# Reordering the mixing stage of a hybrid encoder layer: gate units, state-space steps and GLU units

## The chip, the cores and the metric

The kernel runs on one core of a Trainium2 chip. The metric is the device time of one execution in microseconds. One core has a matrix engine (PE, TensorE), a vector engine (DVE, VectorE), an activation engine (ACT, ScalarE), a general engine (POOL, GpSimd) and a sync engine (SP) that only starts transfers. Each engine runs its own list of instructions in order, and they wait for each other through semaphores, which are counters.

## The reference

One layer works on x of 1024 tokens by 1024 features: a SwiGLU block, a mixing block, a cross-attention and a second SwiGLU block. Only the order inside the mixing block is changed. Cut to what matters:

```python
u = rms_norm(h); p, s, g_pool, g_ssm = split(u @ w_in)      # 512 | 256 | 1024 | 1024
z_pool = (stack_g(pool_minus_self(p[g], window[g]) @ pool_w[g]) * pool_scale) @ w_pool_proj   # 4 groups of 128
y_ssm  = gelu(bidirectional_S5(s))                           # 16 groups of 16 channels, 64 complex states
z_ssm  = (y_ssm @ w_glu_val) * sigmoid(y_ssm @ w_glu_gate)
merged = sigmoid(g_pool) * z_pool + sigmoid(g_ssm) * z_ssm
h = h + merged @ w_mix_out
```

Here pool_minus_self is a centred mean over 2, 4, 8 or 16 tokens less the token itself, and S5 is a linear recurrence forwards and backwards in time.

## The kernel before, in words

Everything is kept transposed, features on the 128 partitions and 1024 tokens along each row. A float32 product is made of three products of shortened parts: weight high by data high, weight high by data low, weight low by data high (`three`, L523 is the matmul in the helper `mm`). A **unit** is one 128x1024 block of weights: SP loads it, POOL splits it into `w_hi` (L1114) and `w_lo` (L1116), and PE runs 48 matmuls of 512 columns with it. There are three slots for split units, so POOL splits a unit as soon as PE has finished the one three before it.

The result of a product goes to one of four PSUM pairs (`take_pair`). PE counts its products, and product k waits until the pair of product k-4 has been read. The readers free the pairs in the order of the products, so DVE must take the products in the order in which PE makes them (`wait_product`).

The mixing block runs in this order on PE:

- four units that make s and the first two groups of p (`opening` and one more);
- the pooled products `pool_mix(g)`, six matmuls each with the data that DVE's `pool(g)` has built by shifted sums, with three units between them: the last two groups of p and the first gate unit (a gate unit is one of eight that make g_pool). DVE scales and splits each result in `pool_mixed(g)`;
- eight steps over pairs of SSM groups. In step q PE runs `ssm_states(q)` (small matmuls on `u_t` and `e_m`), a gate unit, and `ssm_out(q)` (small matmuls on `sx` and `f_m`). Beside the gate unit DVE turns the states and scans them into `sx`. After `ssm_out(q)` DVE copies the result to `y_t`, ACT stores it and starts the six loads of step q+2 (`load_step`) into one of two sets of tables. The last step has a `pool_proj` in place of a gate unit, and three more follow. These loads and the store are issued on ACT's own queue;
- the GLU part, four times: one GLU unit (gate and value products for two of the eight output tiles, four products of 12 matmuls) and two units of g_ssm. DVE and ACT bring them together in `merged`;
- the eight units of w_mix_out, which read `merged` split into `ua_hi` (ACT) and `ua_lo` (DVE), tile by tile. The first of them waits for each tile.

`wait_dve()` on PE or ACT waits for the next count that DVE passes on; `first(tally)` is a tiny memset by which DVE passes one on once its earlier work is done. `link` makes each DVE instruction wait for the one before it.

Of the kernel before, what the change touches and what calls it, by code (L numbers as in the profile page):

```python
# [5 lines left out]
F32 = mybir.dt.float32  # L6
# [5 lines left out]
P = 128  # L12
# [22 lines left out]
KV_BUFFER = (0, 1, 2, 3, 0, 1, 2, 3, 0, 1, 2, 4, 0, 1, 2, 4)  # L35
KP, FP, MP = KT // 2, FT // 2, KT // 2

INV_2PI = float(np.float32(1 / (2 * np.pi)))
# [186 lines left out]
def build(nc, a):  # L225
    ctx = ExitStack()
    with ctx:
# [44 lines left out]
        with ExitStack() as v:  # L272
            merged_again, z_a, z_b, z_c, z_d = tensors(v, [
                ("merged_again", [P, KT, L], F32), ("z_a", [P, 2, L], F32), ("z_b", [P, 2, L], F32),
                ("z_c", [P, L], F32), ("z_d", [P, L], F32)])
        ub_hi, ub_lo = tensors(ctx, [("ub_hi", [P, KT, L], F32R), ("ub_lo", [P, KT, L], F32R)])
# [239 lines left out]
        def _(pe):  # L516
# [326 lines left out]
            def pool_mix(g):  # L843
                pair = take_pair()
                wait_dve()
                three(pair, pw_hi[:, g], pw_lo[:, g], pooled[:, g % 2, 0], pooled[:, g % 2, 1], True, True,
                      HALVES, done=True)

            def ssm_states(q):
# [11 lines left out]
            def ssm_out(q):  # L861
# [4 lines left out]
                for gg in range(2):  # L866
# [15 lines left out]
            pool_mix(3)  # L882

# [6 lines left out]
            for q in range(PAIRS):  # L890
                ssm_states(q)
                if q + 1 < PAIRS:
                    unit_product(ua_hi, ua_lo)
                else:
                    pool_proj()
                ssm_out(q)
            for j in range(1, KT // 2):
                pool_proj()
            wait_dve()
            for j in range(KT // 2):  # L900
                whi, wlo = take_unit()
# [6 lines left out]
                unit_product(ua_hi, ua_lo)  # L908
                unit_product(ua_hi, ua_lo)
            for m in range(KT):  # L910
# [361 lines left out]
        def _(act):  # L1272
# [378 lines left out]
            gate(0)  # L1651
            wait_dve()
            load_step(1)
            for q in range(PAIRS):
                if q + 1 < PAIRS:
                    gate(q + 1)
                wait_dve()
# [13 lines left out]

            for m in range(KT):
                if m % 2 == 0:
                    for m2 in range(2):
                        run(z_b[:, m2], finished_product("glu gate", m + m2)[:].rearrange("p c n -> p (c n)"), ACT.Sigmoid)
                if m == KT - 1:
                    wait_dve()
                    for k in range(5):
                        high(k)
                one(z_d[:], z_c[:], ACT.Sigmoid)  # L1680
            for m in range(5, KT - 1):
                high(m)
            wait_dve()
            high(KT - 1)
            for m in range(KT):
# [62 lines left out]
        def _(dve):  # L1748
# [647 lines left out]
            def pool(g):  # L2396
# [16 lines left out]
                stt(nxt[:, PAD:PAD + L], cur[:, PAD:PAD + L], 1.0 / w, mx_v[:, PAD:PAD + L], ALU.mult, ALU.subtract)  # L2413
                hi, lo = pooled[:, g % 2, 0], pooled[:, g % 2, 1]
                cp(hi, nxt[:, PAD:PAD + L])
# [22 lines left out]

            gate(0)
            link(v.memset(sx[:], 0.0))  # L2440
            dve.wait_ge(s_uld, 16 * T)
            for q in range(PAIRS):
                dve.wait_ge(s_step[q % 2], 96 * (q // 2 + 1))
                tab = step_sets[q % 2][3]
                first(to_pe)
                if q == 0:
                    pool_mixed(2)
                    pool_mixed(3)
                    first()
                    wait_act()  # L2450
                pair = wait_product()
# [20 lines left out]

                if q + 1 < PAIRS:
                    gate(q + 1)
                else:
                    project(0)
                    project(1)
                pair = wait_product()
# [3 lines left out]
                first()  # L2482
                if q + 1 < PAIRS:
                    wait_act()
            for m in range(2, KT):
                if m == KT - 2:
                    wait_act()
                    cp(y_hi[:], y_g[:])
                    tt(y_lo[:], y_g[:], y_hi[:].bitcast(F32), ALU.subtract, tally=to_pe)
                project(m)  # L2490

            def merged_low(m):
# [3 lines left out]

            for m in range(KT):
                if m % 2 == 0:
                    for m2 in range(2):
                        wait_product()  # L2500
                        wait_act()
                        first(free)
                        tt(z_a[:, m2], wait_product(), z_b[:, m2], tally=free)
                pair = wait_product()
                if m == KT - 1:
                    first()
                tt(z_c[:], pair, rn[:], tally=free)
                first()
                if m == KT - 1:
                    for k in range(5):  # L2510
                        merged_low(k)
                wait_act()
                tt(z_d[:], z_d[:], z_a[:, m % 2])
                tt(merged[:, KT - 1 - m], merged[:, KT - 1 - m], z_d[:], ALU.add)
            first()
            for m in range(5, KT):
                merged_low(m)
            dve.wait_ge(s_hload, 16 * KT)
# [145 lines left out]
```

## Time and profile before

| | us |
|---|---|
| median of 3 runs | 2156.42 |
| lowest and highest run | 2152.35, 2160.49 |
| the profiled execution, its own time | 2166.18 |
| its span in the profile | 2164.4 |
| PE busy in the span | 2064.8 (95%) |
| DVE, ACT, POOL busy | 1422.5 (66%), 637.9 (29%), 1218.7 (56%) |

The profiled execution is 9.8 us longer than the median of the runs, and 1.8 us of its time lie outside the span. Times of single instructions come from this execution, counted from the start of the span. The mixing block lies between about 750 and 1246 us.

### The profile page before, as it was taken

To read this page: it belongs to the slowest core of one execution; us is meant where nothing else is said; L and a number is where in the kernel's file an instruction comes from. 1 tells how busy PE (TensorE), PEld (TensorE's weight loads), DVE (VectorE), ACT (ScalarE), POOL (GpSimd) and SP (SyncE) were. 2 spreads that over 40 slices of the span, in tenths; PEclk is the share of its full clock that TensorE was granted. 3 is DMA by queue.
4 is the path that set the end of the run, shared out by engine and by line. 5 is a ranking of instruction groups with operands and counts; after the bars stand their busy time and mean duration, and the time that the engine had idled before them with its cause. 6 is when DMAs were issued, how large, how long until landed. Compare 5 with 4: busy or idle time off the path is not lost.

```text
span 2164.4 us, 24480 instructions
## 1 busy us (share of the span) xinstructions
PE 2064.8 (95%) x9194; PEld 1685.0 (78%) x9194; DVE 1422.5 (66%) x1611; ACT 637.9 (29%) x979; POOL 1218.7 (56%) x802
## 2 busy tenths in 40 slices
PE   8899999999989989999998999899899999999996
PEld 4787778788878877778886888787788888887785
DVE  6677667566776979453334265546677776787778
ACT  5422322233344410001112123324232322234442
POOL 6388687778555532212332431035699998985551
PEclk9999999999999999999999999999999999999998
DMA  6423332347767462332113141111223223267763
GB/s 262 141 95 109 130 133 74 103 140 286 268 223 250 146 172 62 90 98 61 49 49 117 49 160 65 69 58 59 73 93 105 95 93 127 93 223 263 259 213 136
DMA packets 140628, 286.37 MB, mean 132 GB/s; under 512 B 12384, under 2 KB 37600, under 8 KB 140128
## 3 DMA queue, kind: packets, MB, share of 16 engines
q1 hardware_dynamic: 100496, 233.21, 31.7%
q10 hardware_dynamic: 40016, 51.61, 7.4%
q8 instruction: 74, 1.21, 0.2%
q14 instruction: 42, 0.34, 0.0%
HBM read 222.39 MB, written 63.42 MB: 132 GB/s over the span
## 4 chain that ended last, share of the span: by engine, by line
PE 61%; DVE 23%; DMA 6%; issue 4%; POOL 3%; ACT 1%; SPq 1%; DVEq 0%; ACTq 0%; POOLq 0%
PE ps L523 60%; DMA raw<-in_dn 4%; DVE w_lo L2341 3%; DVE xt_lo L2331 3%; DVE f_g L1778 2%; DVE h L2350 2%; DMA d_act<-f_g 1%; DVE acc L1778 1%; DVE sq L2144 1%; POOL w_lo L1106 1%; POOL start_room L1202 1%; DVE ua_lo L1778 1%; DVE sq L2327 1%; DVE sq L2182 1%; POOL raw L1185 1%
## 5 line engine op out<-in xcount | busy, mean ns | idle before, releaser
L1106 POOL TENSOR_TENSOR w_lo<-raw,w_hi 128x512 fp32r<-128x512 f32 x352 | 550.7, 1580 | 221.0 <-ACT w_hi L1341 220.7
L523 PE MATMUL ps<-xt_hi,w_hi 128*128 128x512 f32 x1320 | 517.9, 392 | 12.8 <-DVE xt_lo L2331 11.3
L523 PE MATMUL ps<-xt_lo,w_hi 128*128 128x512 f32 x1320 | 514.1, 389 | 0.0
L523 PE MATMUL ps<-xt_hi,w_lo 128*128 128x512 f32 x1320 | 514.0, 389 | 0.0
L1341 ACT ACTIVATE w_hi<-raw 128x512 fp32r<-128x512 f32 x462 | 278.6, 626 | 534.0 <-POOL raw L1134 269.9
L1114 POOL TENSOR_SCALAR w_hi<-raw 128x1024 fp32r<-128x1024 f32 x54 | 61.4, 1136 | 511.1 <-PE ps L523 504.0
L523 PEld LDWEIGHTS ps<-xt_hi,w_hi 128*128 128x128 f32 x1320 | 248.2, 188 | 75.0 <-issue 20.1
L523 PEld LDWEIGHTS ps<-xt_hi,w_lo 128*128 128x128 f32 x1320 | 248.1, 188 | 52.0
L523 PEld LDWEIGHTS ps<-xt_lo,w_hi 128*128 128x128 f32 x1320 | 248.3, 188 | 50.4
L1134 POOL TENSOR_TENSOR raw<-raw 128x512 f32<-128x512 f32 x178 | 274.6, 1552 | 12.9 <-DMA raw<-in_gu 5.6
L523 PE MATMUL ps<-ua_hi,w_hi 128*128 128x512 f32 x608 | 242.2, 398 | 10.9 <-DVE ua_lo L1778 7.0
L1185 POOL TENSOR_TENSOR raw<-raw 128x512 f32<-128x512 f32 x110 | 164.9, 1509 | 145.1 <-DMA raw<-in_dn 145.0
L523 PE MATMUL ps<-ua_lo,w_hi 128*128 128x512 f32 x608 | 239.9, 394 | 0.0
L523 PE MATMUL ps<-xb_hi,w_hi 128*128 128x512 f32 x528 | 209.1, 396 | 9.7 <-ACT f_g L1434 4.0
L523 PE MATMUL ps<-xb_lo,w_hi 128*128 128x512 f32 x528 | 208.1, 394 | 0.0
L523 PE MATMUL ps<-xb_hi,w_lo 128*128 128x512 f32 x528 | 208.0, 394 | 0.0
L2144 DVE TENSOR_TENSOR f_g<-ps,f_g 128x512 f32<-128x512 f32 x158 | 109.2, 691 | 144.2 <-ACT f_g L1434 119.8
L523 PE MATMUL ps<-ua_hi,w_lo 128*128 128x512 f32 x608 | 189.0, 392 | 0.0
L1116 POOL TENSOR_TENSOR w_lo<-raw,w_hi 128x1024 fp32r<-128x1024 f32 x54 | 145.9, 2702 | 4.5
L523 PEld LDWEIGHTS ps<-ua_hi,w_hi 128*128 128x128 f32 x608 | 116.6, 192 | 39.4 <-DVE ua_lo L1778 5.3
L2341 DVE TENSOR_TENSOR w_lo<-raw,w_hi 128x512 fp32r<-128x512 f32 x110 | 108.8, 989 | 56.2 <-ACT w_hi L1341 55.7
L523 PEld LDWEIGHTS ps<-ua_lo,w_hi 128*128 128x128 f32 x608 | 116.5, 192 | 23.9
(310 smaller groups left out, 2907.6 us busy)
## 6 DMA issues: line engine op xcount, KB each, us to landing
raw<-in_dn SPq DMA_DIRECT2D x264, 256.0 KB, 3.6
raw<-in_gu SPq DMA_DIRECT2D x88, 512.0 KB, 5.6
raw<-in_weights SPq DMA_DIRECT2D x54, 512.0 KB, 3.5
d_act<-acc SPq DMA_DIRECT2D x20, 512.0 KB, 2.8
d_act<-sq SPq DMA_DIRECT2D x20, 512.0 KB, 3.8
d_act<-f_g SPq DMA_DIRECT2D x20, 512.0 KB, 4.6
h<-in_x SPq DMA_DIRECT2D x16, 512.0 KB, 9.1
xt_hi<-d_act SPq DMA_DIRECT2D x8, 1024.0 KB, 7.0
```

The lines of the kernel that those rows point to most:

```text
L523: ins = nc.tensor.matmul(out, lhsT, rhs, start=start, stop=stop)
L1106: add(lo, src, hi.bitcast(F32), op=ALU.subtract).then_inc(s_w_low["pool"], 1)
L1114: nc.gpsimd.tensor_scalar(hi, src, 1.0, 0.0, ALU.mult, ALU.add).then_inc(s_w_hi, 1)
L1116: add(lo, src, hi.bitcast(F32), op=ALU.subtract).then_inc(s_w_low["pool"], 1)
L1134: add(out, x, y, op=op).then_inc(s_w_sum, 1)
L1185: add(raw_part(op, 0), raw_part(op, 0), raw_part(op, 1), op=ALU.add if w[2] > 0 else ALU.subtract).then_inc(s_w_sum, 1)
L1341: nc.scalar.activation(w_hi[:, op.halves[0]].rearrange("p k c -> p (k c)"), src, ACT.Copy).then_inc(s_w_high, 1)
L1778: link(v.tensor_tensor(out, x, y, op), tally)
L2144: link(v.tensor_tensor(out, x, y, ALU.add), adds)
L2331: v.tensor_tensor(xt_lo[:, 3, d % 4], acts_at(d // FP, d % FP), xt_hi[:, 3, d % 4].bitcast(F32), ALU.subtract).then_inc(s_a_lo, 1)
L2341: v.tensor_tensor(lo, raw_part(op, 0), hi.bitcast(F32), ALU.subtract).then_inc(s_w_low["dve"], 1)
L2350: v.scalar_tensor_tensor(out=x, in0=bank, scalar=0.5 * sign, in1=x, op0=ALU.mult, op1=ALU.add).then_inc(s_dev, 1)
```

## The change

It moves instructions and waits; the arithmetic is the same but for the order in which three factors of z_ssm are multiplied. Part by part:

- A unit is put ahead of `pool_mix(0)`, and the second gate unit and `ssm_states(0)` ahead of `pool_mix(3)`. Between the four pooled products PE now has one unit, one unit, and one unit with the small states product. DVE's order follows: `pool(2)` comes before `pool_mixed(0)`, and `pool_mixed(3)` beside step 0.
- `ssm_states(q)` waits for the loads of its step (and `u_t` for q = 0) and for its PSUM pair. The wait for DVE is gone, and with it the count that DVE passed on at the start of each step.
- Gate units run two ahead, so steps 6 and 7 both have a `pool_proj`, and two more follow instead of three. ACT issues the loads of step 1 when `pool_mix(3)` has ended.
- In the GLU part the two units of g_ssm come before the GLU unit, and the packed weights follow. The sigmoid of g_ssm is kept in place (`z_c`), then multiplied by the sigmoid of the GLU gate, then by the value product.
- The high and low splits of `merged` tiles 0 to 3 are put among the work of the last GLU unit.

The diff, cut to its core:

```diff
-        mix += [("glu", j), ("w_in", 14 + 2 * j), ("w_in", 15 + 2 * j)]
+        mix += [("w_in", 14 + 2 * j), ("w_in", 15 + 2 * j), ("glu", j)]
...
             def ssm_states(q):
...
-                wait_dve()
+                if q == 0:
+                    pe.wait_ge(s_uld, 16 * T)
+                pe.wait_ge(s_step[q % 2], 96 * (q // 2 + 1))
...
+            unit_product(ua_hi, ua_lo)
             pool_mix(0)
             unit_product(ua_hi, ua_lo)
             pool_mix(1)
             unit_product(ua_hi, ua_lo)
+            pool_mix(2)
             unit_product(ua_hi, ua_lo)
-            pool_mix(2)
+            ssm_states(0)
             pool_mix(3)
...
             for q in range(PAIRS):
-                ssm_states(q)
-                if q + 1 < PAIRS:
+                if q:
+                    ssm_states(q)
+                if q + EARLY_GATES < KT:
                     unit_product(ua_hi, ua_lo)
                 else:
                     pool_proj()
                 ssm_out(q)
-            for j in range(1, KT // 2):
+            for j in range(EARLY_GATES, KT // 2):
                 pool_proj()
-            wait_dve()
             for j in range(KT // 2):
+                unit_product(ua_hi, ua_lo)
+                unit_product(ua_hi, ua_lo)
+                if j == 0:
+                    wait_dve()
...
             gate(0)
-            wait_dve()
+            act.wait_ge(s_prod, finished["pool mix", 3])
             load_step(1)
...
-            pool(0)
-            pool(1)
+            for g in range(3):
+                pool(g)
             pool_mixed(0)
-            pool(2)
+            pool(3)
             pool_mixed(1)
-            pool(3)
...
-                first(to_pe)
-                if q == 0:
-                    pool_mixed(2)
-                    pool_mixed(3)
...
+            for j in range(KT // 2):
+                last = j == KT // 2 - 1
+                for m2 in range(2):
+                    tt(z_c[:, m2], wait_product(), rn[:], tally=free)
+                    first()
+                for _ in range(2):
+                    wait_act()
+                for m2 in range(2):
+                    m = KT - 1 - (2 * j + m2)
+                    if last:
+                        for k in range(2 * m2, 2 * m2 + 2):
+                            merged_low(k)
+                    wait_product()
+                    wait_act()
+                    first(free)
+                    tt(z_b[:, m2], z_b[:, m2], z_c[:, m2])
+                    tt(z_a[:, m2], wait_product(), z_b[:, m2], tally=free)
+                    tt(merged[:, m], merged[:, m], z_a[:, m2], ALU.add)
...
+            for k in range(4, KT):
+                merged_low(k)
```

On PE at the end of the pooled products, before. The rows are the end of a gate unit (`ua_hi`, `ua_lo`), `pool_mix(2)` and `pool_mix(3)` (`mx_pooled`), `ssm_states(0)` (`u_t`, `e_m`) and the start of the next gate unit:

```order
L523 MATMUL ps<-ua_hi,w_lo 128x512 x2
L523 MATMUL ps<-mx_pooled,pw_hi 128x512 [waits dve_for_pe,psum_pair_free]
L523 MATMUL ps<-mx_pooled,pw_hi 128x512 x3
L523 MATMUL ps<-mx_pooled,pw_lo 128x512 x2
L523 MATMUL ps<-mx_pooled,pw_hi 128x512 [waits dve_for_pe,psum_pair_free]
L523 MATMUL ps<-mx_pooled,pw_hi 128x512 x3
L523 MATMUL ps<-mx_pooled,pw_lo 128x512 x2
L523 MATMUL ps<-u_t,e_m 64x128 [waits dve_for_pe,psum_pair_free]
L523 MATMUL ps<-u_t,e_m 64x128 x7
L523 MATMUL ps<-ua_hi,w_hi 128x512 [waits psum_pair_free,w_lo_written_by_pool]
```

The same place of the change, from the end of the second gate unit:

```order
L524 MATMUL ps<-ua_hi,w_lo 128x512 x2
L524 MATMUL ps<-u_t,e_m 64x128 [waits ssm_step_loaded0,u_loaded,psum_pair_free]
L524 MATMUL ps<-u_t,e_m 64x128 x7
L524 MATMUL ps<-mx_pooled,pw_hi 128x512 [waits dve_for_pe,psum_pair_free]
L524 MATMUL ps<-mx_pooled,pw_hi 128x512 x3
L524 MATMUL ps<-mx_pooled,pw_lo 128x512 x2
L524 MATMUL ps<-ua_hi,w_hi 128x512 [waits psum_pair_free,w_lo_written_by_pool]
```

`pool_mix(2)` and `pool_mix(3)` stood together; now a gate unit and the states product stand between them.

On PE between two steps, before: the end of `ssm_out(0)` (`sx`, `f_m`), then `ssm_states(1)`:

```order
L523 MATMUL ps<-u_t,m_m 128x128
L523 MATMUL ps<-sx,f_m 128x128 x4
L523 MATMUL ps<-u_t,e_m 64x128 [waits dve_for_pe,psum_pair_free]
L523 MATMUL ps<-u_t,e_m 64x128 x7
L523 MATMUL ps<-ua_hi,w_hi 128x512 [waits psum_pair_free,w_lo_written_by_pool]
```

The same place of the change:

```order
L524 MATMUL ps<-u_t,m_m 128x128
L524 MATMUL ps<-sx,f_m 128x128 x4
L524 MATMUL ps<-u_t,e_m 64x128 [waits ssm_step_loaded1,psum_pair_free]
L524 MATMUL ps<-u_t,e_m 64x128 x7
L524 MATMUL ps<-ua_hi,w_hi 128x512 [waits psum_pair_free,w_lo_written_by_pool]
```

The order is the same and the wait for DVE has become a wait for the step's loads.

On DVE at the end of the GLU part, before. `z_c` is the last unit of g_ssm, `ua_lo` the low split of a `merged` tile, and the first row of `h` belongs to the products of w_mix_out:

```order
L1838 MEMSET stat 128x1 [waits product_done,dve_step]
L1778 TENSOR_TENSOR z_c<-ps,rn 128x1024 [waits dve_for_act]
L1838 MEMSET stat 128x1 [waits psum_pair_free]
L1778 TENSOR_TENSOR ua_lo<-merged,ua_hi 128x1024 [waits act_for_dve,dve_for_act]
L1778 TENSOR_TENSOR ua_lo<-merged,ua_hi 128x1024 [waits act_for_dve,dve_for_pe] x4
L1778 TENSOR_TENSOR z_d<-z_d,z_a 128x1024 [waits act_for_dve,dve_for_pe]
L1778 TENSOR_TENSOR merged<-merged,z_d 128x1024 [waits dve_step]
L1838 MEMSET stat 128x1 [waits dve_step]
L1778 TENSOR_TENSOR ua_lo<-merged,ua_hi 128x1024 [waits act_for_dve,dve_for_act]
L1778 TENSOR_TENSOR ua_lo<-merged,ua_hi 128x1024 [waits act_for_dve,dve_for_pe] x2
L2018 SCALAR_TENSOR_TENSOR h<-ps,h 128x1024 [waits product_done,h_reloaded,dve_for_pe]
```

The same place of the change, from the low splits of tiles 2 and 3. The second half of the last GLU unit is `z_b` (gate) and `z_a` (value):

```order
L1787 TENSOR_TENSOR ua_lo<-merged,ua_hi 128x1024 [waits act_for_dve,dve_for_act]
L1787 TENSOR_TENSOR ua_lo<-merged,ua_hi 128x1024 [waits act_for_dve,dve_for_pe]
L1847 MEMSET stat 128x1 [waits act_for_dve,product_done,dve_for_pe]
L1787 TENSOR_TENSOR z_b<-z_b,z_c 128x1024 [waits psum_pair_free]
L1787 TENSOR_TENSOR z_a<-ps,z_b 128x1024 [waits product_done,dve_step]
L1787 TENSOR_TENSOR merged<-merged,z_a 128x1024 [waits psum_pair_free]
L1847 MEMSET stat 128x1 [waits dve_step]
L1787 TENSOR_TENSOR ua_lo<-merged,ua_hi 128x1024 [waits act_for_dve,dve_for_act]
L1787 TENSOR_TENSOR ua_lo<-merged,ua_hi 128x1024 [waits act_for_dve,dve_for_pe] x3
L2027 SCALAR_TENSOR_TENSOR h<-ps,h 128x1024 [waits product_done,h_reloaded,dve_for_pe]
```

Before, five splits stood behind the last `z_c` and three behind the last `merged`. Now four stand beside the last GLU unit and four behind the last `merged`.

## Rows read from the trace of the kernel before

**Rows 1.** The page's busy time, share and instruction count by engine.

```profile
PE 2064.8 (95%) x9194; PEld 1685.0 (78%) x9194; DVE 1422.5 (66%) x1611; ACT 637.9 (29%) x979; POOL 1218.7 (56%) x802
```

**Rows 2.** PE's waits from 797 to 1175 us: in total, times, longest.

```profile
PE ps L523 <- DVE stat L1838: 11.1, 8, 4.6
PE ps L523 <- DVE ua_lo L1778: 7.0, 4, 3.0
```

**Rows 3.** PE by stretch: length, busy (matmuls), granted clock, DMA share, GB/s.

```profile
788.26:799.14 10.88, 10.88 (x49) 1.00 0.49 146
799.14:803.90 4.76, 0.18 (x1) 0.91 0.82 104
803.90:819.08 15.18, 15.13 (x54) 0.80 0.80 132
...
843.56:847.88 4.32, 0.16 (x1) 0.94 0.10 11
847.88:850.71 2.83, 2.83 (x6) 0.50 0.44 168
850.71:851.78 1.07, 1.07 (x18) 0.95 0.00 0
850.71:986.34 135.63, 128.00 (x674) 0.94 0.29 82
983.44:986.34 2.90, 2.90 (x22) 1.00 0.00 0
1149.66:1152.81 3.15, 0.17 (x1) 1.00 0.00 0
1152.81:1170.27 17.46, 13.45 (x48) 0.90 0.43 161
```

**Rows 4.** The same view: states and gate unit of two steps, and `ssm_out(7)`.

```profile
885.52:897.58 12.06, 12.06 (x64) 1.00 0.44 132
901.46:915.09 13.63, 13.62 (x65) 0.87 0.44 117
...
983.43:987.35 3.92, 3.92 (x25) 1.00 0.00 0
```

**Rows 5.** DVE in order of time, pooled part: start, us, instruction, idle before.

```profile
803.97 1.23 DVE L1778 TENSOR_TENSOR mx_v<-ps,rn 128x1024 f32<-128x1024 f32 x1
...
807.07 3.29 DVE L1778 TENSOR_TENSOR mx_b<-mx_a 128x1038 f32<-128x1038 f32 x1
...
814.05 1.28 DVE L1782 TENSOR_SCALAR acc<-ps,pscale 128x1024 f32<-128x1024 f32 x1
...
819.35 1.23 DVE L1778 TENSOR_TENSOR mx_v<-ps,rn 128x1024 f32<-128x1024 f32 x1 [2.03 <-PE ps L523]
...
830.16 1.28 DVE L1782 TENSOR_SCALAR acc<-ps,pscale 128x1024 f32<-128x1024 f32 x1
...
847.77 1.22 DVE L1778 TENSOR_TENSOR merged<-ps,rn 128x1024 f32<-128x1024 f32 x1
...
849.94 1.28 DVE L1782 TENSOR_SCALAR acc<-ps,pscale 128x1024 f32<-128x1024 f32 x1
```

**Rows 6.** The same view, DVE's chain in step 0.

```profile
856.69 0.42 DVE L1778 TENSOR_TENSOR sw<-ps,tab 128x256 f32<-128x256 f32 x1
...
863.57 0.42 DVE L1778 TENSOR_TENSOR sx<-sw 128x256 f32<-128x256 f32 x1
```

**Rows 7.** Loads of `e_m` from 780 to 1000 us, from issue.

```profile
DMA to landing us min/median/max: 2.9/4.9/7.6
```

**Rows 8.** DVE, then ACT, then POOL, in order of time, end of the GLU part.

```profile
1151.44 9.07 DVE L1778 TENSOR_TENSOR ua_lo<-merged,ua_hi 128x1024 fp32r<-128x1024 f32 x5
...
1154.81 1.04 ACT L1278 ACTIVATE z_d<-z_c 128x1024 f32<-128x1024 f32 x1
...
1153.47 1.38 POOL L1114 TENSOR_SCALAR w_hi<-raw 128x1024 fp32r<-128x1024 f32 x1 [10.57 <-PE ps L523]
1154.94 3.23 POOL L1116 TENSOR_TENSOR w_lo<-raw,w_hi 128x1024 fp32r<-128x1024 f32 x1
```

More of the change, by code:

```diff
@@ L36 @@
 KP, FP, MP = KT // 2, FT // 2, KT // 2
+EARLY_GATES = 2
 INV_2PI = float(np.float32(1 / (2 * np.pi)))
@@ L272, in build @@
         with ExitStack() as v:
-            merged_again, z_a, z_b, z_c, z_d = tensors(v, [
-                ("merged_again", [P, KT, L], F32), ("z_a", [P, 2, L], F32), ("z_b", [P, 2, L], F32),
-                ("z_c", [P, L], F32), ("z_d", [P, L], F32)])
+            merged_again, z_a, z_b, z_c = tensors(v, [
+                ("merged_again", [P, KT, L], F32), ("z_a", [P, 2, L], F32), ("z_b", [P, 2, L], F32), ("z_c", [P, 2, L], F32)])
         ub_hi, ub_lo = tensors(ctx, [("ub_hi", [P, KT, L], F32R), ("ub_lo", [P, KT, L], F32R)])
@@ L847, in pool_mix @@
                       HALVES, done=True)
+                finished["pool mix", g] = prod.n
             def ssm_states(q):
@@ L907, in _ @@
                 owed[0] += 1
-                unit_product(ua_hi, ua_lo)
-                unit_product(ua_hi, ua_lo)
             for m in range(KT):
@@ L1651, in _ @@
             gate(0)
-            wait_dve()
+            act.wait_ge(s_prod, finished["pool mix", 3])
             load_step(1)
+            for m in range(1, EARLY_GATES):
+                gate(m)
             for q in range(PAIRS):
-                if q + 1 < PAIRS:
-                    gate(q + 1)
+                if q + EARLY_GATES < KT:
+                    gate(q + EARLY_GATES)
                 wait_dve()
@@ L1670, in high @@
                 run(ua_hi[:, KT - 1 - m], merged[:, KT - 1 - m], ACT.Copy)
[L1672 to L1676, printed above, removed]
+            for j in range(KT // 2):
+                for m2 in range(2):
+                    one(z_c[:, m2], z_c[:, m2], ACT.Sigmoid)
+                for m2 in range(2):
+                    if j == KT // 2 - 1:
+                        for m in range(2 * m2, 2 * m2 + 2):
+                            high(m)
+                    run(z_b[:, m2], finished_product("glu gate", 2 * j + m2)[:].rearrange("p c n -> p (c n)"), ACT.Sigmoid)
+            for m in range(4, KT):
+                if m >= KT - 2:
                     wait_dve()
[L1678 to L1681, printed above, removed]
                 high(m)
-            wait_dve()
-            high(KT - 1)
             for m in range(KT):
@@ L2413, in pool @@
                 stt(nxt[:, PAD:PAD + L], cur[:, PAD:PAD + L], 1.0 / w, mx_v[:, PAD:PAD + L], ALU.mult, ALU.subtract)
+                if g >= 2:
+                    dve.wait_ge(s_prod, finished["pool mix", g - 2])
                 hi, lo = pooled[:, g % 2, 0], pooled[:, g % 2, 1]
@@ L2439, in _ @@
             gate(0)
+            pool_mixed(2)
+            gate(1)
             link(v.memset(sx[:], 0.0))
-            dve.wait_ge(s_uld, 16 * T)
             for q in range(PAIRS):
@@ L2444, in _ @@
                 tab = step_sets[q % 2][3]
-                first(to_pe)
-                if q == 0:
-                    pool_mixed(2)
-                    pool_mixed(3)
-                    first()
-                    wait_act()
                 pair = wait_product()
@@ L2471, in _ @@
                 tt(sx[:, 1, :, 1:], sw[:, 0], sw[:, 1], ALU.add, tally=to_pe)
-                if q + 1 < PAIRS:
-                    gate(q + 1)
-                else:
-                    project(0)
-                    project(1)
+                if q == 0:
+                    pool_mixed(3)
+                if q + EARLY_GATES < KT:
+                    gate(q + EARLY_GATES)
+                else:
+                    if q + EARLY_GATES == KT:
+                        from_act.add(KT - 1)
+                        wait_act()
+                    for m in range(2):
+                        project(2 * (q + EARLY_GATES - KT) + m)
                 pair = wait_product()
@@ L2482, in _ @@
                 first()
[L2483 to L2489, printed above, removed]
+            for m in range(2 * EARLY_GATES, KT):
                 project(m)
+            wait_act()
+            cp(y_hi[:], y_g[:])
+            tt(y_lo[:], y_g[:], y_hi[:].bitcast(F32), ALU.subtract, tally=to_pe)
             def merged_low(m):
@@ L2495, in merged_low @@
                 tt(ua_lo[:, at], merged[:, at], ua_hi[:, at].bitcast(F32), ALU.subtract, tally=to_pe)
[L2497 to L2505, printed above, removed]
-                    first()
[L2507 to L2517, printed above, removed]
+            for j in range(KT // 2):
+                last = j == KT // 2 - 1
+                for m2 in range(2):
+                    tt(z_c[:, m2], wait_product(), rn[:], tally=free)
+                    first()
+                for _ in range(2):
+                    wait_act()
+                for m2 in range(2):
+                    m = KT - 1 - (2 * j + m2)
[3 more added lines that the diff above has]
+                    wait_product()
+                    wait_act()
+                    first(free)
+                    tt(z_b[:, m2], z_b[:, m2], z_c[:, m2])
+                    tt(z_a[:, m2], wait_product(), z_b[:, m2], tally=free)
+                    tt(merged[:, m], merged[:, m], z_a[:, m2], ALU.add)
+                    if last:
+                        first()
+            for k in range(4, KT):
+                merged_low(k)
             dve.wait_ge(s_hload, 16 * KT)
```

## The prediction

> **What bounds the kernel now.** I read the page first: PE is busy for 95% of the span and nothing else is near it [rows 1]. What can be won is time in which PE waits, or runs at the lower of its two clock levels (1.2 instead of 2.4 GHz, a granted clock of 0.5 instead of 1.0). PE's waits from 797 to 1175 us, which hold everything that the change touches, are the second view. Nearly all name DVE: 11.1 us by a count passed on (eight times, the longest 4.6) and 7.0 for `ua_lo` lead the list [rows 2]. The third view cuts PE's time at these places and shows what came after each wait [rows 3]. The reader is to see two things there. A unit at full clock takes 10.88 us for 48 matmuls, 0.227 each. And the stretches behind a wait are longer than their matmuls at that price, at a mean clock of 0.5 to 0.9. A wait here costs itself and then some microseconds at the lower level.
>
> **What can be given back.** Everything is measured from start to start.
>
> (a) Ahead of `pool_mix(0)` PE stands for 4.8 us. The 54 matmuls behind it take 15.1 where 54 x 0.227 is 12.2. Together 7.7 us.
>
> (b) Ahead of `pool_mix(3)` 4.3 us, and its six matmuls take 2.83 instead of 1.36, all at clock 0.50. Together 5.8.
>
> (c) The eight steps take 135.6 us. A step without waits is 1.07 for the states, 10.88 for the unit and 2.90 for the output: 14.85, and 118.8 for eight. Together 16.8. About 7.5 of it is clock: of the seven pieces of states and unit behind a wait, two take 12.1 us and five 13.5 to 13.6 [rows 4], where one of each stands. The other 9.3 are waits, seven times about 1.1 between `ssm_out` and the next states, and once 1.5 for `sx`.
>
> (d) Ahead of the first w_mix_out unit 3.15 us, and that unit takes 17.46 instead of 10.88. Together 9.7.
>
> The sum is 40.0 us [rows 3].
>
> **What the change puts there.** I follow PE from 799.14 with full-clock pieces.
>
> *Opening.* The unit moved ahead runs to 810.0, `pool_mix(0)` to 811.4, a unit and `pool_mix(1)` to 823.6, the first gate unit and `pool_mix(2)` to 835.9, the second gate unit to 846.7, states(0) to 847.8, `pool_mix(3)` to 849.2, the third gate unit to 860.1. DVE had `pooled(0)` ready at 803.97 and `pooled(1)` at 814.05 [rows 5], both well ahead of 810.0 and 822.3. Then `pool(2)` follows at once, for its product ends at 810.0: 10.8 us (819.35 to 830.16), so 824.9, needed at 834.5. `pool_mixed(0)` is 3.3 (two in the 6.75 us from 849.94 [rows 5] to 856.69 [rows 6]), so 828.2. `pool(3)` and `pool_mixed(1)` are 17.6 (830.16 to 847.77) and end at 845.8; the pooled half of it is ready 3.3 us earlier, at 842.5, needed at 847.8. So (a) and (b) vanish. The first gate's copy frees its pair at about 847.1, needed at 847.8 by `pool_mix(3)`: just in time.
>
> *Step 0.* DVE goes on with `pool_mixed(2)` 3.3, the second gate and the memset of `sx` 2.2 (as 847.77 to 849.94), and its chain of 7.3 us (856.69 to 863.57 and 0.42) [rows 5, 6]. That gives `sx` at 847.2 + 3.3 + 2.2 + 7.3 = 860.0, where PE wants it at 860.1. But POOL's splits move with PE. The 3.29 us of an instruction that has 1.23 elsewhere [rows 5] is DVE standing beside a split, about 2.1 us each time. Four such splits are in my durations, and five fall before 851 now. So a wait of 0 to 2.1 us at `ssm_out(0)`, and behind it perhaps half-speed as behind the others, 1.5. I take 1.2 and 1.5, together 2.7.
>
> *Later steps.* PE no longer waits for DVE at the states. DVE needs 0.5 for `y_t`, 7.3 for the chain and 1.3 for the gate out of 14.85, so its chain ends about 3 us before `ssm_out` wants it. The loads of step q+2 start when `y_t(q)` is copied. They are issued over about 4 us and land 2.9 to 7.6 later [rows 7], at most 12 after the copy, and are wanted after 14.4. Those of step 1 start at 849.2 and are wanted at about 863. The rest of (c) is returned. The longer road to the GLU products (two units in place of one `pool_proj`) only adds cover for the reload of y, where PE shows no wait before.
>
> *GLU part.* As much work in another order. Products wait for pairs freed four products earlier, 11 us or more, and DVE has under 10 us of work for 32.6 us of PE. Nothing.
>
> *w_mix_out.* Let T be the end of the last GLU product. The last g_ssm unit ends at T - 10.9. DVE's `z_c` takes it to T - 9.4, two ACT instructions of 1.04 [rows 8] to T - 7.1, when the first high split is there. From there DVE has eleven instructions of 1.26 until the low split of tile 4: T + 7.1. PE wants that tile at T + 4 x 1.36 = T + 5.4: 1.7 us of wait. But the unit behind the last GLU product releases POOL at T, and a split then runs beside DVE. In the kernel before, five low splits took 9.07 us instead of 6.3 beside a split of 3.23 [rows 8], 2.8 more. I take all of it, since POOL starts within a microsecond of T: tile 4 at T + 9.9, a wait of 4.5. Tiles 5 to 7 follow every 1.26, faster than PE's 1.36. With 1.7 for half-speed behind it the cost is 6.2, against 9.7 before.
>
> The Trainium skill, page "SBUF — State Buffer", section "Who interferes with whom", says that the port pair which DVE and GpSimd share is an exclusive lock, held for the whole instruction, so the loser stands fully, and that a vector instruction with two SBUF inputs needs it. By that rule all 4.6 us of POOL's two instructions (1.38 and 3.23) could fall on this chain, a wait of 6.3 and a total 1.8 us higher. The 2.8 us that the trace shows is less, and the sum goes by it.
>
> **Sum.** 40.0 - 2.7 - 6.2 = 31.1 us. The profiled span would be 2164.4 - 31 = 2133. That execution took 2166.18, 9.8 over the median of the runs, and none of this hangs on that difference, so the median goes from 2156.4 to 2125.5. I say 2126.
>
> **The rivals.**
>
> *All of it comes back* (0.15): splits miss DVE at both places, 1.7 left at w_mix_out. 40.0 - 1.7 = 38.3, time 2118. For: with 1.5 instead of 2.1 per stretch `sx` is in time. Against: POOL starts right when DVE's last chain runs.
>
> *The clock does not recover in the steps* (0.17). `ssm_out` and the states are small matmuls of 128 columns, and it may be they, not the waits, after which the clock falls. For: the half-speed stretches come just behind them, also where the wait is only about 1 us, and two equal steps stay at 1.00. Against: `ssm_out(7)` runs with no wait on either side, and it and what follows stand at 1.00 [rows 4]. Then 7.5 us stay: 23.6 saved, 2133.
>
> *DVE is late all along* (0.12): the pooled chain with a stretch more in each of four parts, 4 x 2.1 us, brings 5 to 8 us of wait to `ssm_out(0)`, and `pool_mix(3)` waits for its pair. With the lower clock behind: 22 saved, 2134.
>
> *The step loads become the wait, and it is slower* (0.03). The states now wait for the loads alone. If these, issued in a denser stage and beside POOL's weight traffic, landed later than 14.4 us after `y_t(q)`, each of six steps would be stretched by the excess. It decides against the change from 31 / 6 = 5.2 us of excess on, landings near 20 us; at 22 us it is 6 x 7.6 = 46 lost against 31 won, 2171. Against: 12 us at most in rows of the same loads.
>
> *The orders make no difference in sum* (0.03): PE is throttled or held elsewhere by as much as it gains. 2152. Nothing in the trace speaks for it.
>
> **How the numbers follow.** My forecast has 0.5, with its own range 2121 to 2131 (1.7 to 6.3 at w_mix_out, 0 to 3.6 at step 0, and the spread of the median of three, about 2). The cases at 2118 and 2133 to 2134 take it to 2115 and 2138, with about 0.12 outside. Within 0.5% (10.8 us) is about what this kernel's runs can tell from no change (they spread over 8). Faster by more than that: all but the last two and a little of the others, 0.93. Same 0.04, slower 0.03.
>
> **What would show it.** No wait of PE over 0.3 us from 799 to 860. At most one of 0 to 2 us at `ssm_out(0)`. Steps of 14.8 to 15.0 us from states to states, granted clock 1.00. GLU units in 32.6 us with two g_ssm units each. Ahead of tile 4 of the first w_mix_out unit one wait of 2 to 6 us with DVE's `ua_lo` as releaser, and a low split or a product of two SBUF operands of over 2 us beside POOL's `w_lo`. I am wrong if half-speed stretches stay behind the steps, if the states wait for loads, or if the first pooled products wait for DVE or for a pair.

## The result and the profile after

| | before | after |
|---|---|---|
| median | 2154.39 us (4 runs, 2146.56 to 2160.49) | 2130.11 us (4 runs, 2126.61 to 2134.02) |
| ratio | | 0.9883, 95% interval [0.9857, 0.9909] |
| profiled execution: its own time, span | 2166.18, 2164.4 | 2131.39, 2129.6 |

The change makes the kernel 24.3 us (1.2%) faster. The forecast was 2126, with a range of 2115 to 2138, and a gain of 31 from 2156.4. That median of before had three runs; a fourth (2146.56) took it to 2154.4.

PE's waits after, the view of [rows 2], here from 780 to 1180 us:

```profile
PE ps L524 <- DVE ua_lo L1787: 4.5, 1, 4.5
PE ps L524 <- DVE merged L1787: 1.3, 1, 1.3
PE ps L524 <- DVE sx L1787: 0.7, 1, 0.7
```

Of the eight waits for a count passed on by DVE none is left. Three waits remain, 6.5 us in all. The next view cuts PE's time as [rows 3] did. The columns are the same: stretch, length, busy (matmuls), granted clock, DMA share, GB/s.

```profile
784.56:795.45 10.89, 10.89 (x50) 1.00 0.49 146
795.45:806.33 10.88, 10.88 (x50) 1.00 1.06 116
806.33:807.69 1.36, 1.36 (x8) 1.00 1.00 354
844.30:845.59 1.29, 0.01 (x1) 1.00 0.00 0
845.59:847.12 1.53, 1.53 (x6) 1.00 0.00 0
843.14:966.69 123.55, 121.48 (x679) 1.00 0.33 94
963.79:966.69 2.90, 2.90 (x21) 1.00 0.00 0
1119.14:1136.34 17.20, 12.65 (x49) 0.90 0.51 185
1136.34:1147.22 10.88, 10.88 (x49) 1.00 0.50 191
...
861.98:874.03 12.05, 12.05 (x66) 1.00 0.46 131
876.99:889.05 12.06, 12.06 (x65) 1.00 0.47 130
951.74:963.79 12.05, 12.05 (x65) 1.00 0.20 56
```

The first three rows answer to the first three of [rows 3]: the unit put ahead of `pool_mix(0)` follows at once and the six matmuls behind it take 1.36 us. The fourth and fifth stand at `pool_mix(3)`: a wait of 1.3 instead of 4.3, and 1.53 us instead of 2.83. The sixth is the steps, from `ssm_states(0)` to the end of `ssm_out(7)`. They take 123.6 us, `pool_mix(3)` and its wait (2.8) among them, where they took 135.6 without it. From states to states a step takes 15.0 (861.98 to 876.99). The seventh is `ssm_out(7)`. The three last rows are states and unit of steps 1, 2 and 7, at clock 1.00. The eighth is the first w_mix_out unit: 17.2 us with 4.5 of standing in it, where it took 17.5 with another 3.15 ahead. The ninth is the unit behind it.

### The profile page after: what moved, and what is told of

Read it like the earlier page. It is cut to its first block, busy times and chain, and to the rows that moved or that the text cites. A ratio compares the mean times of both kernels' runs of the same rounds, so it can differ in the third digit from the quotient of the medians.

```text
span 2129.6 us, 24461 instructions
## 1 busy us (share of the span) xinstructions
PE 2051.5 (96%) x9194; PEld 1678.2 (79%) x9194; DVE 1417.6 (67%) x1602; ACT 639.1 (30%) x979; POOL 1225.0 (58%) x802
## 3 DMA queue, kind: packets, MB, share of 16 engines
q8 instruction: 74, 1.21, 0.2%
## 4 chain that ended last, share of the span: by engine, by line
PE 65%; DVE 20%; DMA 5%; POOL 4%; issue 3%; ACT 2%; SPq 1%; DVEq 0%; ACTq 0%; POOLq 0%
PE ps L524 64%; DMA raw<-in_dn 3%; DVE w_lo L2350 3%; DVE xt_lo L2340 2%; DVE f_g L1787 2%; DVE h L2359 2%; POOL w_lo L1114 1%; DMA d_act<-f_g 1%; DVE acc L1787 1%; POOL start_room L1210 1%; POOL raw L1142 1%; DVE sq L2153 1%; POOL raw L1193 1%; DVE ua_lo L1796 1%; DVE ua_lo L1787 1%
```

## The experiments

Three questions were open: what each part of the change gives, what sets the three waits that are left, and why the medians moved by 24 us where the profiled executions differ by 35. Each expectation was written before its kernel ran.

### The changed kernel again, with the granted clock of each run

> The changed kernel once more, for the runs with their granted clocks. Theory A (half-speed stretches explain the spread): over the runs of either kernel, time falls by about 1.06 us for each 0.001 of mean granted clock (2130 us x 0.001 at half level, half of it lost), so the two kernels differ, at equal clock, by only the waits removed: about 9.2 (opening and pool_mix(3)) + 9.3 (steps) - 2 (new waits) + 2.2 or so, 18 to 20 us, and the runs of the kernel before have on average fewer half-speed stretches than its profiled execution. Median difference 22 to 27 us. Theory B (the profiled execution of before was slow for another reason, before or behind the mixing block): time and clock are not tied, and the difference at equal clock is as large as the whole, 24 us or more.

Measured: 2129.92 us (6 runs) against 2154.42 (22 runs of before), ratio 0.9882 [0.9861, 0.9904]. The runs of before spread from 2145.1 to 2164.5, at mean clocks of 0.985 to 0.976. A line through them has 1.5 us for 0.001 of clock with 2.9 us of scatter about it, so a part of theory A holds: clock goes with a part of the spread and by no means all. Mean clock was 0.9809 before and 0.9848 here. At 1.5 us for 0.001 that difference is 5.9 of the 24.5 us, an estimate, and 18.6 are left at equal clock, where theory A had 18 to 20. The profile of this run was the slowest of its six (2138.21). It showed the same three waits. Behind the wait at `ssm_out(0)` it had a stretch of 6.8 us at 1.2 GHz that the first profile had not, and the one at the first w_mix_out unit was 6.8 us long instead of 3.4.

### One part at a time

Only the states' wait, on the kernel before:

```diff
             def ssm_states(q):
...
-                wait_dve()
+                if q == 0:
+                    pe.wait_ge(s_uld, 16 * T)
+                pe.wait_ge(s_step[q % 2], 96 * (q // 2 + 1))
...
-                first(to_pe)
```

> The kernel before with one part of the change: the states products wait for their loads instead of DVE. Theory A (waits and the half-speed behind them are both gone): PE's waits between ssm_out and the states vanish, steps 14.9 to 15.0 us, no half-speed stretch in the steps; 8 waits less of about 1.1, 7.6 us, and 3 to 7.5 us of clock: 11 to 15 us faster. Theory B (the small matmuls lower the clock): 7 to 8 us faster, and half-speed stretches stay in the steps. Theory C (the wait moves to ssm_out, for sx): less than 4 us.

Measured: 2142.16 us (5 runs), 12.3 faster than before, ratio 0.9933 [0.991, 0.9955]. PE's waits are those of before without the seven short ones (6.5 us) and the one for `sx` (1.2):

```profile
PE ps L523 <- DVE ua_lo L1780: 7.0, 4, 3.0
PE ps L523 <- DVE stat L1840: 4.6, 1, 4.6
PE ps L523 <- DVE mx_pooled L1780: 4.2, 1, 4.2
```

The wait did not move to `ssm_out`. That is theory A; theory C is out, and B too, since the waits that went are worth 7.7 us and 12 were won, at least 9.7 by the interval. The clock came back with them: in this profile the mixing block, as the table further down takes it, had 462.3 us of PE busy, where three profiles of before have 464.2 to 470.5, and no half-speed stretch began in the steps.

```profile
750.75:1229.60 478.85, 462.26 (x2157) 0.99 0.29 86
```

Only the GLU part, on the kernel before (the unit order, `z_c` in place, and the splits as in the change's diff):

> The kernel before with one part of the change: gate units ahead of the GLU units and splits beside the last GLU unit. The prediction's sum: 9.7 us become 4.5 of wait at tile 4 of the first w_mix_out unit and 1.7 of half-speed, 3.5 us faster. Rival (this part gives nothing, and all of the change's gain comes from the waits ahead of it): within 1.5 us of before.

Measured: 2153.06 us (10 runs), ratio 0.9982 [0.9966, 0.9998], 1.4 us by the medians and 0.4 to 7.3 by the interval. The wait for `ua_lo` is 4.5 us once instead of 7.0 in four pieces. Both the forecast (3.5) and the rival (within 1.5) lie in the interval, so the runs don't decide between them.

The changed kernel with DVE's count ahead of the states again:

```diff
-                if q == 0:
-                    pe.wait_ge(s_uld, 16 * T)
-                pe.wait_ge(s_step[q % 2], 96 * (q // 2 + 1))
+                wait_dve()
...
             pool_mixed(0)
+            dve.wait_ge(s_uld, 16 * T)
+            dve.wait_ge(s_step[0], 96)
+            first(to_pe)
             pool(3)
...
+                if q:
+                    first(to_pe)
```

> The changed kernel with the wait for DVE put back ahead of the states products. Theory A: the seven waits of 0.9 to 1.1 us between ssm_out and the states return, with half-speed stretches behind some of them: 10 to 15 us slower than the changed kernel, so 10 to 14 us faster than before. Theory C (in the changed order DVE passes its count in time anyway): no slower than the changed kernel by more than 3 us.

Measured: 2147.24 us (8 runs), ratio to before 0.9953 [0.9933, 0.9972], 17 us slower than the change and only 7 faster than before. Theory C is out, and theory A (10 to 15 slower) had the loss too small. PE's waits:

```profile
PE ps L524 <- DVE stat L1845: 10.2, 7, 4.7
PE ps L524 <- DVE ua_lo L1785: 4.5, 1, 4.5
PE ps L524 <- DVE merged L1785: 1.4, 1, 1.4
PE ps L524 <- DVE sx L1785: 0.7, 1, 0.7
```

One of the seven is 4.7 us, which no theory had. In the new order `pool_mixed(3)` and a gate copy stand ahead of `y_t(0)` on DVE, and a states product that waits for DVE waits for all three. So the parts are not independent: of the 17 us, 12 are what the same wait was worth in the old order, and the new order of the pooled part makes it dearer. The other thing to see is the clock behind the waits, in the first three steps:

```profile
864.02:877.53 13.51, 13.51 (x64) 0.88 0.29 79
881.43:893.50 12.07, 12.07 (x65) 1.00 0.45 130
897.38:909.45 12.07, 12.07 (x65) 1.00 0.47 132
```

The clock was low from 860.4 to 867.2, so it fell while PE stood in the wait of 4.7 us (859.3 to 864.0). The wait at `ssm_out(0)` had ended at 856.3, so which of the two it followed is not shown. Behind waits of 0.9, which stand in this execution in six steps, it did not fall. It fell in five of the seven steps with such a wait in the profile of before that the prediction read, in four in the second and in one in the third. This execution was the fastest of its kernel (2134.39; the others lie up to 2150.42).

The changed kernel with the GLU part as before:

> The changed kernel with the GLU part as before (GLU unit first, five low splits behind the last sigmoid's copy). From the kernel with this part alone, which was 0.2% faster than before: 2 to 6 us slower than the changed kernel, PE's waits ahead of and in the first w_mix_out unit 3.0 and 4.0 again. Rival (the other parts need the new GLU order, for instance for the reload of y): more than 8 us slower, with a wait at the first GLU unit.

Measured: 2136.83 us (4 runs), ratio to before 0.991 [0.9874, 0.9946], 6.9 slower than the change by the medians, with intervals that overlap, where 2 to 6 were expected. PE waits 5.7 us for `ua_lo` in three pieces (3.0, 0.5 and 2.2) instead of 4.5 in one, and for nothing at the first GLU unit. So the rival's wait did not come; its time, more than 8 us, the interval alone would not exclude. In this profile the mixing block took 466.3 us, within the 464.5 to 468.6 of the change, so most of the 6.9 is not found in it.

### What sets the wait at the first w_mix_out unit

```diff
                 for name, count in op.after:
                     pool.wait_ge(released[name], count)
+                if op.key == stage_units()[1].index(("mix_out", 2)):
+                    pool.wait_ge(s_prod, finished["first mix_out"])
```

> The changed kernel, with one wait more on POOL: it splits the third w_mix_out unit only when the first w_mix_out product is done, so no split runs beside DVE's last splits of merged. Theory A (the wait at tile 4 is DVE's chain plus its standing beside POOL's split): PE's wait for ua_lo falls from 4.5 to about 1.7 us, no ua_lo over 1.3 us, and the half-speed behind it mostly goes, 2.8 to 4.5 us faster than the changed kernel, near 2127. Theory B (the wait is the chain's length alone): the wait stays at 4 us or more and the time does not move.

Measured: 2127.61 us (4 runs), ratio to before 0.9867 [0.9837, 0.9896]. PE's wait for `ua_lo` is 1.9 us instead of 4.5. The views to compare are DVE and POOL in order of time at this place. In the changed kernel:

```profile
1118.79 3.21 DVE L1787 TENSOR_TENSOR ua_lo<-merged,ua_hi 128x1024 fp32r<-128x1024 f32 x2
1122.06 0.06 DVE L1847 MEMSET stat<- 128x1 f32 x1
1122.16 3.18 DVE L1787 TENSOR_TENSOR z_b<-z_b,z_c 128x1024 f32<-128x1024 f32 x1
1125.37 1.23 DVE L1787 TENSOR_TENSOR z_a<-ps,z_b 128x1024 f32<-128x1024 f32 x1
...
1119.72 1.21 POOL L1122 TENSOR_SCALAR w_hi<-raw 128x1024 fp32r<-128x1024 f32 x1 [7.34 <-PE ps L524]
1121.01 3.24 POOL L1124 TENSOR_TENSOR w_lo<-raw,w_hi 128x1024 fp32r<-128x1024 f32 x1
```

and with the late split:

```profile
1116.15 2.48 DVE L1791 TENSOR_TENSOR ua_lo<-merged,ua_hi 128x1024 fp32r<-128x1024 f32 x2
1118.70 0.06 DVE L1851 MEMSET stat<- 128x1 f32 x1
1118.80 1.23 DVE L1791 TENSOR_TENSOR z_b<-z_b,z_c 128x1024 f32<-128x1024 f32 x1
1120.06 1.22 DVE L1791 TENSOR_TENSOR z_a<-ps,z_b 128x1024 f32<-128x1024 f32 x1
...
1129.90 1.05 POOL L1126 TENSOR_SCALAR w_hi<-raw 128x1024 fp32r<-128x1024 f32 x1 [20.15 <-PE ps L524]
```

Without the late split POOL's two instructions stand beside three of DVE. `z_b` ends at 1125.34, 1.09 us after `w_lo` (1124.25), and takes 1.23 when alone: it did nearly all its work behind `w_lo`. Two low splits went from 3.21 to 2.48 us and the product of two SBUF operands from 3.18 to 1.23: 2.7 us less on DVE, 2.6 less of PE's wait. The split was the cause, and what is left is the chain's length, 1.9 where the count of eleven instructions gave 1.7. Theory B is out. No half-speed stretch is left in the mixing block. In the median 2.3 us were won against 2129.92, where 2.8 to 4.5 were expected, within what these runs can tell from nothing.

With the chain begun earlier:

```diff
+                    if j == KT // 2 - 1 and m2 == 1:
+                        act.wait_ge(s_prod, finished["last w_in"])
+                        high(0)
                     one(z_c[:, m2], z_c[:, m2], ACT.Sigmoid)
...
-                for _ in range(2):
-                    wait_act()
+                wait_act()
+                if last:
+                    merged_low(0)
+                wait_act()
```

> The late split, and ACT and DVE start the first high and low split before the second sigmoid of g_ssm, about 2.3 us earlier. By the count of instructions behind the last g_ssm unit (DVE's chain starts at T - 9.4 instead of T - 7.1, T being the end of the last GLU product): tile 4 ready at about T + 5.4 as PE wants it, a wait of 0 to 0.5 us and no half-speed there. Total 4.5 us of wait and 1.6 us or more of half-speed less than the changed kernel: about 6 us, near 2124. Rival (the value product sets the chain: z_a, merged, high and low of tile 7 in a row behind T): a wait of 1 to 2 us appears at tile 7 instead and 3 to 4 us are won.

Measured: 2122.68 us (4 runs), ratio to before 0.9846 [0.9815, 0.9877]. The wait for `ua_lo` is 1.6 us instead of 1.9. The expected 0 to 0.5 was not met: the second low split now stood beside POOL's split of the unit before and took 2.43 us, and DVE idled 0.9 ahead of it for ACT, whose second high split stood behind a sigmoid. The two take 2.1 of the 2.3 us by which the chain began earlier. The wait is still at tile 4, so the rival, a wait at tile 7, did not come. The median is 4.9 lower than with the late split alone and 7 under the change, where about 6 were expected. Of the 4.9 the wait explains 0.3. The rest is not explained by anything in this stage, and the intervals overlap.

### The waits at the opening, and the fastest version

On top of the two edits before:

```diff
+                if op.key in (9, 10):
+                    pool.wait_ge(s_prod, finished["pool mix", 3] if op.key == 9 else finished["gate 2"])
```

> The kernel with early splits of merged and a late split on POOL, and the splits of the fourth and fifth gate units late as well: the first waits for pool_mix(3), the second for the third gate unit. In the changed kernel's profile the split beside pool(3) makes two DVE instructions 2.8 us longer, and PE waits 1.3 us at pool_mix(3) for the pair of the first gate copy, and 0.7 at ssm_out(0). Theory A (the count of DVE's instructions plus the split beside it sets both): the 1.3 us go, at ssm_out(0) 0 to 0.8 stay, and the half-speed stretch near 860 comes less often: 1.3 to 4 us less than splits_early. Theory B (DVE is late by its own length): both waits stay, no change. The control: no new wait of PE for POOL's w_lo.

Measured: 2120.16 us (5 runs), ratio to before 0.9832 [0.9803, 0.986]. One wait of PE is left from 780 to 1200 us (0.8 us for `ua_lo` at the start of the block, near 755, stand in every profile and are in no list of waits here):

```profile
PE ps L524 <- DVE ua_lo L1799: 1.6, 1, 1.6
```

In the changed kernel, `pool(3)` on DVE had the first two of these rows beside POOL's split, which is the last two:

```profile
832.01 1.96 DVE L1787 TENSOR_TENSOR mx_a<-mx_b 128x1036 f32<-128x1036 f32 x1
834.00 3.31 DVE L1787 TENSOR_TENSOR mx_b<-mx_a 128x1032 f32<-128x1032 f32 x1
...
831.39 1.50 POOL L1122 TENSOR_SCALAR w_hi<-raw 128x1024 fp32r<-128x1024 f32 x1 [7.61 <-PE ps L524]
832.97 3.25 POOL L1124 TENSOR_TENSOR w_lo<-raw,w_hi 128x1024 fp32r<-128x1024 f32 x1
```

They do not slow each other evenly, they take turns. DVE's first row ends at 833.97, 1.08 us behind `w_hi` (832.89). `w_lo` ends at 836.22, 2.25 behind that row, and takes 2.40 alone. DVE's second row ends at 837.31, 1.09 behind `w_lo`. The same distances, to 0.05 us, stand at the other such meetings in the mixing block of this profile, 15 for a `w_lo` and 14 for a DVE row of this size in all. One more DVE row, which writes in another order (`s_perm`) and takes 2.02 with an operand in PSUM, ends 1.88 behind.

With that split late DVE's two rows are:

```profile
829.99 1.24 DVE L1799 TENSOR_TENSOR mx_a<-mx_b 128x1036 f32<-128x1036 f32 x1
831.26 1.23 DVE L1799 TENSOR_TENSOR mx_b<-mx_a 128x1032 f32<-128x1032 f32 x1
```

2.8 us less, and both waits (1.3 and 0.7) are gone, with no new wait for `w_lo`. Theory A holds and B is out. In the median 2.5 us were won against the kernel before this edit, as expected (1.3 to 4), but within what these runs can tell from nothing. This kernel is the fastest of the case, 36 us under the runs of before taken beside it. The last 10 of them, from 2130 to 2120, came with edits that only move splits in time; no work was taken away. In the mixing block 8.4 of the 10 are seen against the mean of three profiles of the change: 5.0 of waiting and 3.4 of clock.

### Three profiles of each kernel

> The kernel before, profiled again, for the half-speed time in its mixing block. Theory A (the profile that the prediction read had more of it than most executions): waits of PE from 797 to 1175 as before, 23 to 24 us, but less than 30.7 us of half-speed between the first w_in product and the first w_q product, 15 to 27, and that stretch 2 to 8 us shorter than 494.7. Theory B (it is the same each time): within 1.5 us of 494.7.

> The kernel before, a third profile. Waits of PE from 797 to 1175 us again 22 to 24 us; half-speed in the mixing block 20 to 34 us; the mixing block 488 to 495 us; the rest of the program within 1656 to 1670 us. If the rest varies by more than the mixing block, most of the spread of runs, and of the 9.8 us between the profile read for the prediction and the median, lies outside the block.

> The changed kernel, a third profile. Waits of PE in the mixing block again 6.5 us; half-speed there 3 to 14 us (3.4 and 13.7 in the two so far), the block 464 to 469 us. If it is again above 3.4, the clock term that the changed kernel keeps is larger than the 3.2 us that the prediction gave it.

These single executions took 2153.30, 2153.38 and 2129.32 us. The table is PE's view of the mixing block, from the first matmul on `ua_hi` to the first on `ub_hi`, in every profile. Waiting is length less busy.

| | block | PE busy | PE waiting | rest of the span |
|---|---|---|---|---|
| before, read for the prediction | 494.72 | 470.49 | 24.2 | 1669.7 |
| before, second | 491.78 | 468.59 | 23.2 | 1659.7 |
| before, third | 487.06 | 464.23 | 22.8 | 1664.5 |
| after | 464.47 | 457.05 | 7.4 | 1665.1 |
| after, second | 468.58 | 461.18 | 7.4 | 1667.8 |
| after, third | 465.11 | 457.67 | 7.4 | 1662.4 |
| fastest version | 457.66 | 455.23 | 2.4 | 1657.1 |

The third profile of before and the second of after, as the view by stretch has them:

```profile
750.00:1237.06 487.06, 464.23 (x2158) 0.98 0.28 84
```

```profile
748.26:1216.84 468.58, 461.18 (x2157) 0.99 0.29 87
```

The waiting is nearly the same each time: 22.8 to 24.2 us before, 7.4 after. The busy time for the same matmuls is not, for it contains the microseconds at 1.2 GHz: 464.2 to 470.5 before, 457.1 to 461.2 after. By the granted clock the block holds 30.7, 27.3 and 17.1 us at 1.2 GHz in the three profiles of before, 3.4, 13.7 and 6.8 in those of after, and none in the fastest version. Theory A of the second profile of before holds for the length (491.8 and 487.1, 3 to 8 less than 494.7), and just about for the half-speed time (15 to 27 expected). The third was below what was expected in both (487.1 for 488 to 495, 17.1 for 20 to 34). The third of after was as expected. The block's means are 491.2 and 466.1, so 25.1 us less: 16.0 of waiting and 9.1 of clock. That is close to the difference of the medians (24.3 and 24.5). The rest of the span, which the change doesn't touch, differs by 10 us among the three of before, the block by 7.7.

## Why the prediction was right, and where it was off

**The bound and the four places.** Right but for one place. PE's waits and the lower clock behind them were what could be won, and in the opening, in the steps and at w_mix_out they changed as said. At `pool_mix(3)` a wait of 1.3 for a PSUM pair stayed. By the prediction's own signs this was one against it: no wait over 0.3 us from 799 to 860, and no pooled product that waits for a pair. The pooled products wait no more for their data, steps take 15.0 us at clock 1.00, and GLU units 32.6 us with their two g_ssm units (in the first profile of after).

**The new waits.** At tile 4 of the first w_mix_out unit 4.5 us were forecast and 4.5 measured. The two parts of it, 1.7 of chain and 2.8 beside POOL's split, were taken apart by the late split: 1.9 and 2.6. (Eleven instructions of 1.26 are 13.9 and end at T + 6.8; the T + 7.1 of the sum needs the four small memsets between them, 0.1 each, which it doesn't name.)

The 6.3 us that the prediction drew from an exclusive lock did not come, but the lock is not what was wrong. The Trainium skill, page "SBUF — State Buffer", section "Who interferes with whom", has it as a lock, and the rows of DVE and POOL above agree: each instruction ends a fixed time behind the other's end, to 0.05 us. The step from the lock to 4.6 us failed. POOL's instructions stand too, for the DVE instruction that is under way when they start: of their 4.45 us here 1.0 is that (1.21 and 3.24, against 1.05 and 2.40 alone), and DVE works in that time. DVE lost 2.7.

At `ssm_out(0)` 1.2 were forecast and 0.7 measured. At `pool_mix(3)` the pair of the first gate copy was called "just in time" and costed at nothing. It cost 1.3. The reason is the one named for `sx` in the next paragraph, a fifth split beside DVE, which was not added there. That split costs more, too, than the 2.1 us counted: 2.8 here, since it meets two DVE instructions. The prediction priced the row of 3.29 at 807.07 and not the one ahead of it.

**The steps.** Right, with the case that put the fall of the clock on the small matmuls refused: three profiles of the changed kernel have between them one step at 1.2 GHz, behind the wait at `ssm_out(0)` in one. The six loads of a step never made PE wait. One size was off: the eight steps without waits were put at 118.8 us and are 120.0 here (123.6 less 2.8 for `pool_mix(3)` and 0.7 of wait), so 1.2 of the 16.8 could not come back.

**The clock term.** This is the step that failed in size: "none of this hangs on that difference, so the median goes from 2156.4 to 2125.5". The sum was made in one execution and carried over whole. Its waiting may be carried over, for that is the same each time: 17.7 us of it were to go on balance (23.4, length less busy in [rows 3], against 5.7), and on the mean of three profiles each 16.0 went. Its clock may not. The profile that was read had 470.5 us of PE busy in the block, and the mean of three is 467.8. Against the 455.2 of the fastest version, which has no half-speed stretch there, that is 15.3 and 12.6 us of clock. The changed kernel has 1.8 to 6.0, on the mean 3.4, and the forecast had 3.2 (1.5 and 1.7). So the term was right for the kernel after and, as a mean, too large by 2.7 for the one before. In the pair of profiles the block shrank by 30.2 us, close to the 31.1 of the sum; on the mean of three each it is 25.1. The 9.8 us between that profile's time and the median lay in part in the block, 3.5 over its mean of three, and in part outside, 5.1 over the mean of the rest of the span, where the change has no hand.

**The range and chances.** The main case's own range of 2121 to 2131 holds the 2130 measured, at its upper end. That the time came within 4 us where the gain was off by 7 is in part luck: the median of three runs that it started from was 2.0 above that of four. The case of DVE late all along, with 2134, is as near in time and occurred only in small part: `pool_mix(3)` waits for its pair, as it said, but its 5 to 8 us at `ssm_out(0)` are 0.7. The case in which all comes back, with 2118, is the kernel with the splits moved: 2120, with 1.6 of wait left where that case had 1.7. That the times agree to 2 us is luck in part, for that case has the same clock term, and the kernel also begins its splits earlier.

## What to carry to other kernels

Count a wait of the matrix engine at its own length in every execution, but take the price of the clock behind it from several profiles, or as a range from nothing to what one profile shows. When an in-order engine feeds PE with work from several places, let each product wait for what it reads and not for a count that stands behind other work: the same reordering won 24 us with that and 7 without, and 12 of these 17 us came from that alone in the old order. A split or copy that can wait 10 us should not start when it can but when the engine that it holds up has no urgent work. To see such a hold-up, compare ends and not lengths: an instruction that ends a fixed time behind another engine's has stood for it.

## What the hardware showed beside this

- VectorE instructions of two SBUF operands (128x1024, 1.23 us alone) and GpSimd's splits (`w_hi` 1.05, `w_lo` 2.40 alone) did not overlap but took turns. One that started while the other engine's ran ended a fixed time behind it: VectorE's 1.07 to 1.12 us behind GpSimd's end, `w_lo` 2.25 to 2.27 and `w_hi` 0.91 to 0.93 behind VectorE's. So one of VectorE takes up to 3.3 us and a `w_lo` up to 3.5, and each of the two splits that were moved had cost VectorE 2.7 to 2.8 us. Instructions that read PSUM were not held and held nothing (`merged` at 844.31 took 1.22 us beside `w_hi`, and `acc` at 845.69 took 1.28 beside a `w_lo` of 2.40). A cast of one SBUF operand was: 1.20 us at 847.01 instead of 0.69.
- Waits of the same 0.9 us were followed by 1.2 GHz in five, four and one of seven steps in three executions of the kernel before, and in none of six in one of the kernel with the count put back. Single waits of 4 us and more had it in them or right behind them in every profile read here, and so had the group of waits in the first w_mix_out unit that came to 5.7 us and more. What decides for the short ones stays open.
- Executions of one kernel on one core spread by 19 us (2145 to 2164 in 22 runs). The mean granted clock goes with a part of it, and about 3 us of scatter about the line remain. The waits of the mixing block, the same within 1.4 us in three profiles, don't account for it.
